# Two 64-wide heads on separate halves of the array in layer two's attention, and its loop written out

## The chip, the cores and the metric

The kernel runs on 1 core of one Trainium2 chip. The metric is the time of one execution on the device in microseconds, the median over runs. Engines are called TensorE (PE; PEld for its weight loads), VectorE (DVE), ScalarE (ACT), GpSimd (POOL) and SyncE (SP, which here issues the DMAs).

## The reference

Two transformer blocks run one after the other on x (256 positions x 2048), all in fp32. The first has two layers: latent attention, then sliding-window attention. The second is one layer with block attention, a state-space mixer and a gated feed-forward network. The change is in the sliding-window layer: 32 query heads of 64 dimensions share 4 key/value heads (8 query heads to one), in two blocks of 128 queries. A query block sees its own keys and those of the block before, within a window of 128, and each head has a sink logit in its softmax.

```python
qb = q.reshape(B, nb, BLOCK, SWA_KV_HEADS, SWA_GROUP, D)
kw, vw = band(k), band(v)
s = jnp.einsum('bnqhgd,bnkhd->bnhgqk', qb, kw).astype(jnp.float32) * (D ** -0.5)
valid = (diff >= 0) & (diff < SWA_WINDOW) & (key_abs >= 0)
s = jnp.where(valid[None, :, None, None], s, NEG_INF)
m = jnp.maximum(jnp.max(s, axis=-1, keepdims=True), sink)
e = jnp.exp(s - m)
p = e / (jnp.sum(e, axis=-1, keepdims=True) + jnp.exp(sink - m))
o = jnp.einsum('bnhgqk,bnkhd->bnqhgd', p.astype(v.dtype), vw)
...
x = x + (y * jax.nn.silu(gate)) @ w_out
```

## The kernel before

**Weight tiles.** All large products stream weights from HBM in tiles of 128 x 1024 fp32. SP loads a tile into one of four slots (`load`, L367), ScalarE casts it to `w_high` (fp32r), VectorE makes the remainder `w_low` (L1458), and TensorE multiplies high by high, high by low and low by high (`block_b`, L445, with 128 x 128 weights and 256 streamed columns; `block_a`, L454). A slot is free when TensorE has used the tile. One tile in the form of `tile_b` is 24 matmuls.

**Layer two.** After the keys and values (L658 to L676) come four projection steps and one step of the output projection. `swa_step(i, project, attend)` (L704) is one: a projection step multiplies 16 tiles (8 for the queries of a group of 8 heads, 8 for their gate) and, placed by hand between the tiles, does the attention of the four head pairs m = 0 to 3 of the group projected in the step before. Step 0 projects only, steps 1 to 3 (the loop at L793) do both, step 4 attends only and has tiles of the output projection in place of the projection's. So 16 pairs are attended, p = 4(i-1) + m. VectorE, ScalarE and POOL run the same steps, with loops of their own (L1779, L1261, L2102), in orders written out by hand.

For each pair TensorE does three things, in this order around the tiles:
- `swa_scores` (L678): for each of the two heads the products of query block 0 with 128 keys and of query block 1 with 256 keys, into that head's own PSUM bank of `sc`, and then one matmul of the identity with the masks (fp32r, 384 columns). The queries of a pair lie in `qs[:, m, :]`, head 0's 64 dimensions on partitions 0 to 63, head 1's on 64 to 127. The keys are placed for each head (`kz`, filled by ScalarE at L1192): head h's 64 partitions hold the keys, the other 64 are zeros (L1661). So each product runs over 128 rows, half of them zeros.
- `probs_transposed` (L516): six transposes of the normalised probabilities, when VectorE has them (`p_ready`).
- `swa_values` (L692): the output of both heads, summed into one bank. `vz`, placed by POOL (L2096), holds head h's values in its 64 of 128 columns and zeros in the others, so head 0's product writes zeros into head 1's output partitions and the other way round, and head 1's is added on top.

The order on TensorE in steps 1 to 3 is scores(0), tiles 0 to 2, flipped(0), tile 3, scores(1), values(0), tiles 4 to 6, flipped(1), tile 7, scores(2), values(1), tiles 8, 9, the rotation of the new queries (four matmuls of 512 columns in all, L740), tile 10, flipped(2), tile 11, scores(3), values(2), tiles 12 to 14, flipped(3), tile 15, values(3). Scores(0) of the next step follows values(3) directly. In step 4 there are two tiles between a scores block, with the values block behind it, and the transposes of the same pair.

All fp32 products and the masks go through one helper, `f32mm` (L485, L486), so they share the line L486 in the profile; they are told apart by their tiles (`scores<-k_swa_placed,q_swa`, `scores<-identity_and_masks`, `bank<-prob_T,v_swa_placed`). Transposes are L489. The softmax of a pair (`row_maxima`, `exponentials`, `normalised` on VectorE and ScalarE) starts on `s_ready`, which the last mask signals.

Layer three (the second block) has in its loop a product `ssm_bcast` (L818) with 16 rows of weights, 128 columns and 512 streamed columns (`bank<-gate,gate_tanh`), and ahead of it one of 33 rows by 8 columns (L816, `bank<-constants,rel_bias`).

Of the kernel before, what the change touches and what calls it, by code (L numbers as in the profile page):

```python
# [31 lines left out]
P = 128  # L32
SEQ = 256
# [117 lines left out]
def after(eng, sem, count):  # L151

    eng.wait_ge(sem, count + 1)
# [23 lines left out]
def program(nc, a, out, toeplitz):  # L177
# [3 lines left out]
    def sb(name, shape, dt=F32, where=None):  # L181
        return (where or persistent).enter_context(nc.sbuf_tensor(name, shape, dt))
# [4 lines left out]
    with ctx:  # L187
# [28 lines left out]
        pT = sb("prob_T", [P, 2, 384], F32, att)  # L216
# [34 lines left out]
        kz = sb("k_swa_placed", [P, SWA_KV, 2, SEQ], F32, a3)  # L251
        vsw = sb("v_swa", [P, TT, SWA_KV * SWA_D], F32, a3)
        vz = sb("v_swa_placed", [P, TT, 2, P], F32, a3)
        qsr = sb("q_swa_raw", [P, 4, SEQ], F32, a3)
        qs = sb("q_swa", [P, 4, SEQ], F32, a3)
# [34 lines left out]
        sc = ctx.enter_context(nc.psum_tensor("scores", [P, 2, 512], F32))  # L290
        b6 = ctx.enter_context(nc.psum_tensor("bank6", [P, 512], F32))
        b7 = ctx.enter_context(nc.psum_tensor("bank7", [P, 512], F32))
        banks = [bank[0][:, :], bank[1][:, :], bank[2][:, :], bank[3][:, :], sc[:, 0, :], sc[:, 1, :],
                 b6[:, :], b7[:, :]]
# [143 lines left out]
        def _(pe):  # L438
# [6 lines left out]
            def block_b(to, tile, cols, chunk, act_h, act_l, first, last):  # L445

                s = tile % SLOTS
                wh, wl = whi[s][:, :], wlo[s][:, :]
                h, l = cols(wh), cols(wl)
                nc.tensor.matmul(to, h, act_h[:, chunk, :], start=first, stop=False, skip_group_check=True)  # L450
                nc.tensor.matmul(to, h, act_l[:, chunk, :], start=False, stop=False, skip_group_check=True)  # L451
                return nc.tensor.matmul(to, l, act_h[:, chunk, :], start=False, stop=last, skip_group_check=True)  # L452

            def block_a(to, tile, cols, chunk, t, act_h, act_l, first, last):  # L454

                s = tile % SLOTS
                h, l = cols(whi[s][:, :]), cols(wlo[s][:, :])
                ah, al = act_h[:, chunk, t * P:(t + 1) * P], act_l[:, chunk, t * P:(t + 1) * P]
                nc.tensor.matmul(to, ah, h, start=first, stop=False, skip_group_check=True)  # L459
                nc.tensor.matmul(to, ah, l, start=False, stop=False, skip_group_check=True)  # L460
                return nc.tensor.matmul(to, al, h, start=False, stop=last, skip_group_check=True)  # L461

            def span(first, n):
                return lambda w: w[:, first:first + n]
# [20 lines left out]
            def f32mm(to, lhsT, rhs, start=True, stop=True):  # L485
                return nc.tensor.matmul(to, lhsT, rhs, start=start, stop=stop, skip_group_check=True)  # L486

            def flip(to, rows_in_):
                return nc.tensor.transpose(to, rows_in_, ident)  # L489
# [40 lines left out]
            for slot, n in enumerate((V_SLOT0, 48, 2 * FC, 2 * FC, 2 * FC, 2 * FC)):  # L530
                last = nc.tensor.transpose(banks[slot // 3][:, (slot % 3) * P:(slot % 3) * P + n], rows[0:n, slot, :], ident[0:n, 0:n])
# [15 lines left out]
            for b in range(4):  # L547
                for c in range(2):
                    for t in range(TT):
                        k = 2 * b + c  # L550
                        last = flip(banks[b][:, c * SEQ + t * P:c * SEQ + (t + 1) * P], c_sb[:, t, k * P:(k + 1) * P])
# [106 lines left out]
            for j in range(8):  # L658
                pe.wait_ge(hl_done, max(8 + j + 1, 8 + 2))
                ready(T_KV + j)  # L660
                for at in range(2):
# [3 lines left out]
                    for t in range(TT):  # L665
                        last = block_a(banks[1][:, t * SEQ:(t + 1) * SEQ], T_KV + j, span(at * 512 + 256, 256), 2 * j + at,
                                       t, hTh, hTl, j + at + t == 0, 2 * j + at == DC - 1)
# [4 lines left out]
            for g in range(SWA_KV):  # L672
                last = f32mm(banks[g][:, 0:SEQ], cst[:, C_DUP + (g % 2) * P:C_DUP + (g % 2 + 1) * P], krot[:, g // 2, :])
# [4 lines left out]
            def swa_scores(i, m):  # L678

                p = 4 * (i - 1) + m  # L680
                after(pe, sw["q_placed"], i)
                after(pe, sw["exp_done"], p)
                after(pe, sw["pt1_sb"], p)
                for h in range(2):
                    for first, q, nk in ((0, 0, P), (P, 1, SEQ)):
                        keys = (kz[:, i - 1, h, 0:nk] if isinstance(i, int) else
                                kz[:, bass.ds(i - 1, 1), h, 0:nk].rearrange("p o n -> p (o n)"))
                        f32mm(sc[:, h, first:first + nk], qs[:, m, q * P:(q + 1) * P], keys, q == 0, False)
                    last = f32mm(sc[:, h, 0:384], ident_r, mask_band, False, True)
                last.then_inc(sw["s_ready"], 1)  # L690

            def swa_values(i, m):  # L692
                p = 4 * (i - 1) + m
                after(pe, sw["pt0_sb"], p + 1)
                after(pe, sw["pt1_sb"], p + 1)
                after(pe, sw["vz"], i)
                after(pe, sw["y32_done"], p)
                for h in range(2):
                    f32mm(banks[7][:, 0:SEQ], vz[:, 0, h, :], pT[:, h, 0:SEQ], h == 0, False)
                for h in range(2):  # L700
                    last = f32mm(banks[7][:, P:SEQ], vz[:, 1, h, :], pT[:, h, SEQ:384], False, h == 1)
                last.then_inc(sw["o_ready"], 1)

            def swa_step(i, project, attend):  # L704
# [19 lines left out]
                def scores(m):  # L724
                    if attend:
                        swa_scores(i, m)
# [5 lines left out]
                def values(m):  # L732
                    if attend:
                        swa_values(i, m)
# [55 lines left out]
                tiles(12, 13, 14, 15)  # L790

            swa_step(0, True, False)
            with pe.Fori(1, 4) as i:  # L793
                swa_step(i, True, True)
            swa_step(4, False, True)
            last_groups(T_SWAO, GROUPS_OUT[1])
# [13 lines left out]
            for c in range(DC):  # L810
                last = block_b(banks[2][:, 0:SEQ], T_DT, span(c * SSM_H, P), c, hTh, hTl, c == 0, c == DC - 1)
# [1380 lines left out]
```

## Time and profile before

| | |
|---|---|
| Median of 3 runs | 2000.13 us (1999.19 to 2002.28) |
| The profiled execution | 2002.27 us, span 2000.1 us |
| TensorE busy | 1907.7 us, 95% of the span, 13112 matmuls |
| VectorE, ScalarE, GpSimd busy | 1110.5, 896.9, 151.3 us |
| Granted clock of TensorE, mean share | 0.982 |
| HBM traffic | 321 MB read, 162 GB/s over the span |
| Layer two, steps 1 to 3 | 486.4 to 673.2 us of the span |

The span is the stretch from the first to the last instruction that the profiler recorded; the execution's own time lies around it. TensorE's matmuls are pipelined, so records of neighbours overlap: a matmul of 256 columns is shown with 0.28 us and the next starts 0.12 us later. What one costs is read from start to start. A row of the time order is: start, duration, engine, line, operation, output<-inputs by the program's names, rows*columns of the weights, the streamed operand, count; several like instructions in a row are merged (x4, x8), and a bracket tells of idle time ahead and of what ended it. A short window shows them singly.

### The profile page before, as it was taken

What the parts mean: (1) busy time and instruction counts of PE and PEld (TensorE: products, weight loads), DVE (VectorE), ACT (ScalarE), POOL (GpSimd) and SP (SyncE); (2) the same over time, 40 slices, a digit from 0 to 9 for tenths busy, and PEclk for the clock granted to TensorE, in tenths of its full rate; (3) what the DMA queues carried; (4) which work ended last, traced back from release to release, by engine and by line L of the source; (5) the groups of instructions that cost most, each with busy time, mean ns of one, the idle gap of its engine ahead of it and who ended that gap; (6) DMA issues with size and microseconds to landing.
All of it is one profiled execution on the core that took longest, in us unless ns stands there. A gap on an engine that the chain in (4) does not pass through costs nothing.

```text
span 2000.1 us, 35228 instructions
## 1 busy us (share of the span) xinstructions
PE 1907.7 (95%) x13112; PEld 1771.1 (89%) x13112; DVE 1110.5 (56%) x1575; ACT 896.9 (45%) x1347; POOL 151.3 (8%) x177
## 2 busy tenths in 40 slices
PE   6899999889999997999999997999999999999997
PEld 5799998789999875999999786999999999988885
DVE  6555565545565655665555555556555556544444
ACT  5454444444444444454344444454444444433333
POOL 1001110000011000000000000100000000023322
PEclk9899999999999998999999998999999999999999
DMA  6455545535444454455554453555556555555553
GB/s 215 144 149 144 154 153 168 168 116 160 146 132 131 127 161 143 127 161 170 157 156 144 163 189 122 183 181 185 181 180 186 179 182 185 180 184 185 187 188 115
DMA packets 234781, 324.11 MB, mean 162 GB/s; under 512 B 12272, under 2 KB 170116, under 8 KB 234080
## 3 DMA queue, kind: packets, MB, share of 16 engines
q1 hardware_dynamic: 233296, 317.63, 51.0%
q0 software_dynamic: 1136, 4.58, 0.7%
q10 hardware_dynamic: 288, 1.09, 0.2%
q8 instruction: 39, 0.64, 0.1%
q14 instruction: 22, 0.18, 0.0%
HBM read 321.14 MB, written 2.11 MB: 162 GB/s over the span
## 4 chain that ended last, share of the span: by engine, by line
PE 92%; DVE 3%; ACT 2%; issue 1%; DMA 1%; POOL 0%; ACTq 0%; DVEq 0%; SPq 0%
PE bank L450 17%; PE bank L451 17%; PE bank L452 17%; PE bank L459 7%; PE bank L461 7%; PE bank L460 7%; PE bank L486 4%; PE bank L1002 3%; PE bank L1001 3%; PE bank L1003 3%; PE scores L486 3%; PE scores L1002 1%; PE scores L1001 1%; PE scores L1003 1%; PE bank L489 1%
## 5 line engine op out<-in xcount | busy, mean ns | idle before, releaser
L1458 DVE TENSOR_TENSOR w_low<-raw,w_high 128x1024 fp32r<-128x1024 f32 x603 | 739.3, 1229 | 756.2 <-ACT w_high L1025 755.7
L1025 ACT CAST w_high<-raw 128x1024 fp32r<-128x1024 f32 x603 | 630.2, 1048 | 828.9 <-PE bank L452 467.5
L450 PE MATMUL bank<-hT_high,w_high 128*128 128x256 f32 x2672 | 765.4, 286 | 8.8 <-issue 3.1
L451 PE MATMUL bank<-hT_low,w_high 128*128 128x256 f32 x2672 | 758.4, 284 | 0.0
L452 PE MATMUL bank<-hT_high,w_low 128*128 128x256 f32 x2672 | 758.4, 284 | 0.0
L450 PEld LDWEIGHTS bank<-hT_high,w_high 128*128 128x128 f32 x2672 | 515.4, 193 | 11.8 <-issue 11.4
L451 PEld LDWEIGHTS bank<-hT_low,w_high 128*128 128x128 f32 x2672 | 515.4, 193 | 1.1 <-issue 1.0
L452 PEld LDWEIGHTS bank<-hT_high,w_low 128*128 128x128 f32 x2672 | 515.2, 193 | 0.0
L459 PE MATMUL bank<-w_high,yT_high 128*128 128x512 f32 x384 | 152.9, 398 | 1.9 <-POOL yT_low L2076 1.9
L461 PE MATMUL bank<-w_high,yT_low 128*128 128x512 f32 x384 | 152.4, 397 | 0.0
L460 PE MATMUL bank<-w_low,yT_high 128*128 128x512 f32 x384 | 151.1, 394 | 0.0
L459 PE MATMUL bank<-w_high,hT_high 128*128 128x256 f32 (+1 forms) x352 | 107.6, 306 | 0.0
L460 PE MATMUL bank<-w_low,hT_high 128*128 128x256 f32 (+1 forms) x352 | 106.4, 302 | 0.0
L461 PE MATMUL bank<-w_high,hT_low 128*128 128x256 f32 (+1 forms) x352 | 106.3, 302 | 0.0
L1001 PE MATMUL bank<-w_high,hidden_high 128*128 128x512 f32 x264 | 104.1, 394 | 1.3 <-DVE up_conv L1994 1.3
L1002 PE MATMUL bank<-w_low,hidden_high 128*128 128x512 f32 x264 | 105.3, 399 | 0.0
L1003 PE MATMUL bank<-w_high,hidden_low 128*128 128x512 f32 x264 | 103.5, 392 | 0.0
L459 PEld LDWEIGHTS bank<-w_high,yT_high 128*128 128x128 f32 x384 | 72.1, 188 | 18.8 <-POOL yT_low L2076 1.6
L461 PEld LDWEIGHTS bank<-w_high,yT_low 128*128 128x128 f32 x384 | 72.1, 188 | 17.5
L460 PEld LDWEIGHTS bank<-w_low,yT_high 128*128 128x128 f32 x384 | 72.1, 188 | 17.4
L459 PEld LDWEIGHTS bank<-w_high,hT_high 128*128 128x128 f32 x352 | 67.2, 191 | 8.5 <-issue 6.1
L461 PEld LDWEIGHTS bank<-w_high,hT_low 128*128 128x128 f32 x352 | 67.2, 191 | 2.5
(270 smaller groups left out, 2022.6 us busy)
## 6 DMA issues: line engine op xcount, KB each, us to landing
raw<-in_w_up SPq DMA_DIRECT2D x176, 512.0 KB, 4.5
raw<-in_w_in SPq DMA_DIRECT2D x88, 512.0 KB, 3.5
raw<-in_w_down SPq DMA_DIRECT2D x88, 512.0 KB, 3.5
raw<-in_w_swa SPq DMA_DIRECT2D x72, 512.0 KB, 3.5
raw<-in_w_c SPq DMA_DIRECT2D x50, 512.0 KB, 3.8
raw<-in_w_mlao SPq DMA_DIRECT2D x32, 512.0 KB, 3.8
raw<-in_w_swao SPq DMA_DIRECT2D x32, 512.0 KB, 4.1
raw<-in_w_out SPq DMA_DIRECT2D x32, 512.0 KB, 3.6
```

Source lines behind the costliest of these rows:

```text
L450: nc.tensor.matmul(to, h, act_h[:, chunk, :], start=first, stop=False, skip_group_check=True)
L451: nc.tensor.matmul(to, h, act_l[:, chunk, :], start=False, stop=False, skip_group_check=True)
L452: return nc.tensor.matmul(to, l, act_h[:, chunk, :], start=False, stop=last, skip_group_check=True)
L459: nc.tensor.matmul(to, ah, h, start=first, stop=False, skip_group_check=True)
L460: nc.tensor.matmul(to, ah, l, start=False, stop=False, skip_group_check=True)
L461: return nc.tensor.matmul(to, al, h, start=False, stop=last, skip_group_check=True)
L486: return nc.tensor.matmul(to, lhsT, rhs, start=start, stop=stop, skip_group_check=True)
L1001: nc.tensor.matmul(to, ah, whi[s][:, w], start=first, stop=False, skip_group_check=True)
L1002: nc.tensor.matmul(to, ah, wlo[s][:, w], start=False, stop=False, skip_group_check=True)
L1003: last = nc.tensor.matmul(to, al, whi[s][:, w], start=False, stop=True, skip_group_check=True)
L1025: nc.scalar.copy(whi[s][:, :], raw[s][:, :]).then_inc(high_made, 1)
L1458: v.tensor_tensor(wlo[s][:, :], raw[s][:, :], whi[s][:, :].bitcast(F32), ALU.subtract).then_inc(low_made, 1)
```

## The change

In `swa_scores` each head's products use only its own 64 partitions of queries and keys (`half`), so 64 rows of the array, and the heads alternate inside each query block; the masks follow both. In `swa_values` each head's product takes only its own 64 columns of `vz` and writes only its own 64 output partitions (`dims`), each with a start of its own. TensorE's loop over steps 1 to 3 becomes Python's, so that its code is written out three times with constant addresses. Nothing else differs: `kz` and `vz` are filled as before, and the other engines keep their loops.

```diff
@@ swa_scores
+                for first, q, nk in ((0, 0, P), (P, 1, SEQ)):
+                    for h in range(2):
+                        half = slice(64 * h, 64 * h + 64)
+                        f32mm(sc[:, h, first:first + nk], qs[half, m, q * P:(q + 1) * P], kz[half, i - 1, h, 0:nk],
+                              q == 0, False)
                 for h in range(2):
-                    for first, q, nk in ((0, 0, P), (P, 1, SEQ)):
-                        keys = (kz[:, i - 1, h, 0:nk] if isinstance(i, int) else
-                                kz[:, bass.ds(i - 1, 1), h, 0:nk].rearrange("p o n -> p (o n)"))
-                        f32mm(sc[:, h, first:first + nk], qs[:, m, q * P:(q + 1) * P], keys, q == 0, False)
                     last = f32mm(sc[:, h, 0:384], ident_r, mask_band, False, True)
                 last.then_inc(sw["s_ready"], 1)
@@ swa_values
                 for h in range(2):
-                    f32mm(banks[7][:, 0:SEQ], vz[:, 0, h, :], pT[:, h, 0:SEQ], h == 0, False)
+                    dims = slice(64 * h, 64 * h + 64)
+                    f32mm(banks[7][dims, 0:SEQ], vz[:, 0, h, dims], pT[:, h, 0:SEQ], True, False)
                 for h in range(2):
-                    last = f32mm(banks[7][:, P:SEQ], vz[:, 1, h, :], pT[:, h, SEQ:384], False, h == 1)
+                    dims = slice(64 * h, 64 * h + 64)
+                    last = f32mm(banks[7][dims, P:SEQ], vz[:, 1, h, dims], pT[:, h, SEQ:384], False, True)
                 last.then_inc(sw["o_ready"], 1)
@@ the steps
             swa_step(0, True, False)
-            with pe.Fori(1, 4) as i:
+            for i in range(1, 4):
                 swa_step(i, True, True)
             swa_step(4, False, True)
```

## Rows read from the trace of the kernel before

**Rows 1.** The page: chain that ended last, share of the span by engine.

```profile
PE 92%; DVE 3%; ACT 2%; issue 1%; DMA 1%; POOL 0%; ACTq 0%; DVEq 0%; SPq 0%
```

**Rows 2.** One pass: length, busy time and count by engine, PEclk, DMA share.

```profile
548.70:610.90 62.20, 62.20 (x486) 60.41 (x485) 38.21 (x75) 28.15 (x63) 6.01 (x10) 1.00 0.44 135
```

**Rows 3.** Who waited for whom, 428 to 745 us: total, times, longest.

```profile
ACT w_high L1025 <- PE bank L452: 90.6, 51, 3.7
...
PE bank L489 <- DVE prob L1507: 5.1, 5, 1.8
...
PE bank L450 <- issue: 3.1, 1, 3.1
```

**Rows 4.** Chain that ended last, 480 to 745: start, us, what.

```profile
500.98 1.67 PE scores L486 x10
502.64 1.31 PE bank L486 x8
```

**Rows 5.** TensorE in order of time, one values block: start, duration, what.

```profile
502.48 0.38 PE L486 MATMUL bank<-prob_T,v_swa_placed 128*128 128x256 f32 x1
...
502.70 0.59 PE L486 MATMUL bank<-prob_T,v_swa_placed 128*128 128x256 f32 x2
...
503.34 0.50 PE L486 MATMUL bank<-prob_T,v_swa_placed 128*128 128x128 f32 x3
...
503.45 0.50 PE L486 MATMUL bank<-prob_T,v_swa_placed 128*128 128x128 f32 x3
```

**Rows 6.** TensorE in order of time, end of one pass, next start.

```profile
547.95 1.47 PE L486 MATMUL bank<-prob_T,v_swa_placed 128*128 128x256 f32 x8
549.25 0.82 PE L486 MATMUL scores<-k_swa_placed,q_swa 128*128 x4
...
550.09 0.82 PE L486 MATMUL scores<-k_swa_placed,q_swa 128*128 x4
...
550.91 0.28 PE L450 MATMUL bank<-hT_high,w_high 128*128 128x256 f32 x1
```

**Rows 7.** In order of time, the 16-row block: TensorE, then its weight loads.

```profile
912.06 0.28 PE L452 MATMUL bank<-hT_high,w_low 128*128 128x256 f32 x1
912.27 1.12 PE L486 MATMUL bank<-gate,gate_tanh 16*128 16x512 f32 x2
913.32 0.39 PE L459 MATMUL bank<-w_high,hT_high 128*128 128x256 f32 x1
913.54 0.28 PE L460 MATMUL bank<-w_low,hT_high 128*128 128x256 f32 x1
...
912.80 0.59 PE L486 MATMUL bank<-gate,gate_tanh 16*128 16x512 f32 x1
...
912.27 0.29 PEld L486 LDWEIGHTS bank<-gate,gate_tanh 16*128 16x128 f32 x2
913.32 0.19 PEld L459 LDWEIGHTS bank<-w_high,hT_high 128*128 128x128 f32 x1 [0.76 <-issue]
```

**Rows 8.** TensorE in order of time, the rotation; its group by line and shape.

```profile
524.57 0.28 PE L452 MATMUL bank<-hT_high,w_low 128*128 128x256 f32 x1
...
526.53 0.28 PE L451 MATMUL bank<-hT_low,w_high 128*128 128x256 f32 x1
...
L486 PE MATMUL bank<-q_swa_raw,constants 128*128 128x512 f32 x16 | 7.5, 592 | 0.0
```

**Rows 9.** TensorE in order of time, the block of 33 rows by 8 columns.

```profile
884.28 0.28 PE L452 MATMUL bank<-hT_high,w_low 128*128 128x256 f32 x1
884.49 0.81 PE L486 MATMUL bank<-constants,rel_bias 33*8 33x384 f32 x2
...
885.45 0.28 PE L451 MATMUL bank<-hT_low,w_high 128*128 128x256 f32 x1
```

**Rows 10.** TensorE in order of time, waits of transposes, first pass and last step.

```profile
497.24 0.55 PE L489 MATMUL bank<-constants,prob 128*128 128x128 f32 x3 [0.32 <-DVE prob L1507]
...
696.99 0.55 PE L489 MATMUL bank<-constants,prob 128*128 128x128 f32 x3 [0.98 <-DVE prob L1507]
```

## The prediction

> **What bounds the kernel now.** I read the page first, then the stretches of layer two, then the chain that ended last inside them, and last TensorE's order of time. The page gives TensorE 92% of the chain that ended last [rows 1]. In layer two the same holds more sharply: the middle one of three like passes lasts 62.2 us and TensorE is busy in all of it, at the full clock of 2.4 GHz (granted share 1.00), while VectorE and ScalarE are busy for some 38 and 28 us [rows 2]. The producers of weight tiles wait for TensorE and not the reverse: ScalarE's cast waits 90.6 us for slots that TensorE frees. TensorE itself waits 5.1 us there, five times, for the normalised probabilities [rows 3]. So a microsecond less on TensorE in a loop pass is a microsecond less in the end, and one more is one more, unless it lies beside those five waits.
>
> The two blocks that change stand in the chain as pieces: a scores block takes 1.67 us, a values block 1.31 [rows 4]. There are 16 of each (pairs 0 to 15), 47.7 us together. That is all the change can touch.
>
> **What a block is made of.** An fp32 product is two TensorE instructions, each with its own weight load: a values block with four products is eight matmuls. Those that stream 256 columns start 0.22 us apart (502.48, 502.70), those of 128 columns 0.11 apart (503.34, 503.45) [rows 5]. So the four products of a values block are 4 x 0.216 + 4 x 0.11 = 1.30. A scores block holds the same number of instructions of the same widths, 1.30, and two masks: a head takes 0.83, its half of the products 0.65, its mask 0.18 [rows 6].
>
> **Part one: changing the array's shape.** The new products use 64 rows (scores) or 64 output columns (values); masks, transposes and weight tiles use the whole array. No row of before has this pair of shapes, but a block in layer three has 16 rows by 128 columns, between two whole-array tiles. From the last whole-array start before it (912.06) to the second one behind it (913.54) is 1.48 us; off go 0.12 each for two ordinary neighbours and 2 x 0.43 for its two matmuls of 512 columns (twice the 0.216 of 256): 0.38, say 0.40 with the roundings [rows 7]. The rotation block of layer two, four such matmuls in the whole array, goes from 524.57 to 526.53, 1.96 us, and 1.96 - 0.24 - 4 x 0.43 = 0.00 [rows 8]. So it is the shape and not the kind of work that costs. It has two halves of 0.20: the load comes 0.21 behind the last start instead of at the next matmul's heels (0.09 of pause, then 0.11 of a load that nothing hides), and the same on the way back (the second matmul begins at 912.80 and streams until 913.23, the load is at 913.32, and the matmul proper, 0.12 ahead of its successor at 913.54, 0.10 later). A block of 33 rows by 8 columns goes from 884.28 to 885.45, 1.17; less 0.24 and 2 x 0.32 (384 columns) leaves 0.29 [rows 9]: with 8 columns to load, the exposed load on the way in is nearly gone, the rest stays. For 64 columns I take the middle, 0.35.
> - Scores: in and out, 16 x 0.40 = 6.4 us (bounds 0.29 to 0.40 a block).
> - Values: in and out, 0.35 a block (0.29 to 0.40).
> - Where values(3) of one pass runs straight into scores(0) of the next, the way out and in is one change and not two: three places, -0.6 us.
>
> The Trainium skill has the same rule ("TensorEngine Tiling (Array Packing)", Key Properties): a change of tiling mode drains TensorE, a change of tile within a mode doesn't. It speaks against this change, and the trace agrees, with the 0.09 pauses above; it gives no price.
>
> **Part two: what the halves may save.** Nothing in the trace of before has two matmuls at once, so this is bounded from both sides: nothing (the products take their 1.30), or half (0.65). Fewer rows alone save nothing: the second 16-row matmul of 512 columns lasts 0.59 [rows 7], the 128-row ones of the rotation 592 ns on average [rows 8]. All that can be saved is saved by running the two heads side by side. Which value I take follows from the order written: both instructions of head 0's product come before both of head 1's, and in every view starts follow program order. So I let a matmul start as soon as the one before it has started and its own half is free. Values: 0, 0.216; head 1 at 0.22, 0.436; then the narrow ones at 0.44, 0.55, 0.65, 0.76, the end at 0.87. That saves 0.43 of 1.30. Scores: by the same rule 0.87, but each of the eight also needs 128 columns of weights, and two loads of 128 columns start no closer than 0.11: the pair of 0.29 in all, of which one lasts 0.18 or 0.19 [rows 7]; a load one by one delays the second half of the stairs, 0, 0.11, 0.22, 0.33, 0.44, 0.656, 0.66, 0.876, the end at 1.09. That saves 0.21. I take 1.09: the loads are spaced 0.11 with 16 rows as with 128. Were loads of different halves made side by side, the scores would end at 0.87 as well; no row shows two loads at once. The loads of values have 64 columns and keep up either way.
>
> The Trainium skill (same page and section) says that different tiles can load weights in parallel. No run here has shown it yet; it is the second of these two cases.
>
> **The sum.** Scores: 0.40 - 0.21 = +0.19 a block, all on the path (the softmax chain starts when they end), 16 x 0.19 = +3.0. Values: 0.35 - 0.43 = -0.08. In the last step three values blocks lie between a scores block and transposes that wait for that same softmax chain, 0.98 us each time [rows 10], so what they gain or lose is swallowed: 13 x -0.08 = -1.0. Merged changes -0.6. **Together +1.4 us.** With loads side by side the scores save 0.43, 16 x -0.03 = -0.5 in place of +3.0, and the sum is -2.1.
>
> The other edits cost nothing. The loop written out: at the pass boundary values(3) starts at 547.95 and scores(0) 1.30 later, with the masks and tiles at their usual distance, so branch and register arithmetic already lie beside matmuls [rows 6]. If fetching longer code stalled TensorE, the one unexplained wait of the stretch, 3.1 us, is my upper bound, and as a gain, were that wait the loop's, it is the lower [rows 3]. I take 0, since the steps before and behind the loop are already written out without such waits. POOL, DVE and ScalarE instructions, DMAs and semaphores are the same; the zeros in the placed keys and values are still written, and nobody waits for them newly. A transposition in a pass has three tiles (8.6 us) and the values block ahead of it and is late but once, by 0.32, where no values block is ahead of it [rows 10]; 0.08 less changes that not at all. If TensorE got much faster, the next to be late would be those same probabilities.
>
> The profiled execution took 2002.27 us around a span of 2000.1; the median of the three runs is 2000.13. The profile is thus at the upper end of them, and I add +1.4 to the median: **2001.5 us** (2003.7 against the profiled one).
>
> **The rivals.**
> - *No overlap.* The halves are used one after the other, because fp32 instructions or the order keep TensorE strictly serial. Products stay at 1.30 and each block pays its change of shape: 16 x 0.40 + 13 x 0.35 - 0.6 = +10.4, **2010.5 us**, slower. Place: every scores block and thirteen values blocks. It decides once overlap saves less than 0.40 in a scores block or 0.35 in a values block. For it: no two matmuls run together anywhere in the trace; the saving needs something never seen here. Against: separate rows or columns hold separate weights, and nothing in the data forbids it. If only one of the kinds overlaps, it is +4.8 (values only: 6.4 - 1.0 - 0.6) or +7.0 (scores only: 3.0 + 4.6 - 0.6).
> - *Stairs with loads side by side.* As above, -2.1, **1998.0 us**. For it: the halves' weights lie apart. Against: loads of few rows and of many are spaced alike.
> - *Full overlap.* Head 1 starts with head 0 whatever was written between: 0.65 saved in both. 16 x (0.40 - 0.65) + 13 x (0.35 - 0.65) - 0.6 = -8.5, **1991.6 us**, faster. For it: the two heads share no half. Against: the order, and starts in program order in every view. The Trainium skill (same page, Theoretical Speedup) speaks of up to twice the speed for a dimension of 64; no row here shows a doubling.
> - *The change doesn't do what it says.* 64 rows or columns run as an idle part of the whole array, no change of shape, no overlap: 0.0, **2000.1 us**. Against: the 16- and 33-row blocks both pay.
>
> **How the numbers follow.** Stairs with loads one by one, the forecast: 0.32 (own range 1999 to 2004, +-1 for roundings and more for the runs' own spread). Stairs with loads side by side: 0.15. No overlap, or in one kind alone: 0.37. Full overlap: 0.11. No change of shape: 0.05. These need 1996 to 2012 for 8 in 10, with full overlap outside. A measurement of this kernel tells apart about 0.2%, 4 us. Both kinds of stairs lie inside that band, as does the unchanged shape; full overlap is faster; no overlap or a single kind is slower. Faster 0.12, same 0.50, slower 0.38.
>
> **What would show it.** In the profile after: matmuls of scores<-k_swa_placed with 64 rows and of bank<-prob_T with 64 columns. Load starts 0.09 late at each change and a first whole-array matmul of 0.39 behind. A scores block of about 1.86 in the chain (0.40 + 1.09 + 0.36) instead of 1.67, a values block of about 1.22 instead of 1.31, and a pass of 62.2 + 4 x 0.19 - 4 x 0.08 - 0.2, some 62.4. No overlap: 2.06 and 1.65, a pass near 65. Full overlap: 1.41 and 1.00, a pass near 59.8. Head 1's first matmul starting while head 0's second still streams is the step on which all hangs. I am wrong if blocks pay no pause, if a pass boundary costs or gains over 0.3 us, or if the transpositions of the passes begin to wait.

## The result and the profile after

The changed kernel takes 1991.69 us (median of 5 runs, 1989.95 to 1994.15), the kernel before in the same series 2002.28 (1999.19 to 2005.20). The ratio is 0.9948, 95% interval 0.9931 to 0.9965: **faster by 0.5%**, some 10 us. The forecast was 2001.5 with a range from 1996 to 2012: wrong, and outside the range. The measured time is that of the rival with full overlap (1991.6), which had a chance of 0.11. That the two agree to 0.1 us is in part luck: the rival counted from a median of 2000.13, and the same kernel has 2002.28 in this series.

The page of the changed kernel: busy time by engine, one DMA queue, the chain by engine.

```profile
PE 1898.3 (95%) x13112; PEld 1748.6 (88%) x13112; DVE 1110.7 (56%) x1575; ACT 895.5 (45%) x1347; POOL 151.5 (8%) x177
...
q8 instruction: 47, 0.77, 0.2%
...
PE 92%; DVE 3%; ACT 2%; issue 1%; DMA 1%; POOL 0%; SPq 0%; DVEq 0%; ACTq 0%
```

TensorE's share of the chain is the same 92% as in [rows 1]; the span fell from 2000.1 to 1991.1 us. The queue that brings instructions has 47 packets where it had 39. That is the loop written out (the run with the loop alone has 47 too), and it shows nowhere else.

Where the time went is read best between two marks that both kernels have: the first rotation matmul of step 0 and the first transpose behind layer two. First the kernel before, then the changed one, the latter with one pass besides, from the second to the third step's rotation (length, busy time and count by engine, PEclk, DMA share, GB/s).

```profile
467.47:797.55 330.08, 311.41 (x2082) 284.51 (x2081) 191.23 (x344) 146.63 (x298) 25.98 (x46) 0.99 0.46 142
```

```profile
467.22:789.24 322.02, 302.02 (x2082) 261.85 (x2081) 191.22 (x344) 145.44 (x298) 26.02 (x46) 0.98 0.48 146
...
583.32:643.30 59.98, 59.97 (x487) 54.93 (x486) 38.18 (x76) 27.87 (x61) 6.03 (x10) 1.00 0.48 141
```

330.08 became 322.02: 8.06 us of the 9.0 of the two profiled spans lie in layer two. The rest comes from outside the change: 0.25 us before the stage and some 0.7 behind it. The mean granted clock doesn't explain it (0.982 before and 0.981 after), and no run shows its cause. A pass is 59.98 us, where it was 62.2 [rows 2].

The chain in the changed kernel, a scores block, the values block behind it and the next tile's first matmul:

```profile
500.72 1.40 PE scores L486 x10
502.13 0.80 PE bank L486 x8
502.93 0.32 PE bank L450
```

1.67 and 1.31 [rows 4] became 1.40 and 0.80; the 0.32 of the first whole-array matmul holds 0.20 that belong to the way out of the values block, so 1.00 in all. The rival had said 1.41 and 1.00.

Now TensorE in order of time in the same place, one short window and its weight loads below it:

```profile
500.44 0.28 PE L452 MATMUL bank<-hT_high,w_low 128*128 128x256 f32 x1
500.65 0.93 PE L486 MATMUL scores<-k_swa_placed,q_swa 64*128 64x128 f32 x8
501.51 0.62 PE L486 MATMUL scores<-identity_and_masks 128*128 128x384 f32 x2
502.06 0.87 PE L486 MATMUL bank<-prob_T,v_swa_placed 128*64 128x256 f32 x8
502.86 0.39 PE L450 MATMUL bank<-hT_high,w_high 128*128 128x256 f32 x1
503.08 0.28 PE L451 MATMUL bank<-hT_low,w_high 128*128 128x256 f32 x1
...
500.65 0.38 PE L486 MATMUL scores<-k_swa_placed,q_swa 64*128 64x128 f32 x2
...
500.65 0.19 PEld L486 LDWEIGHTS scores<-k_swa_placed,q_swa 64*128 64x128 f32 x2
```

Three things are to be seen. The shape has changed (64\*128, 128\*64), and a change looks as in [rows 7]: the last matmul of the tile ends its columns at 500.44 + 0.12 = 500.56, the first load of the new shape comes at 500.65, and a first matmul of 0.39 stands behind the last change. From 500.44 to 503.08 it is 2.64 us for the pair of blocks; in the kernel before the same way took 3.22 (500.69 to 503.91), 0.58 more. The eight score matmuls are over in 0.93 us with their pipeline's tail, where one head's four took 0.82 [rows 6]. And at 500.65 there are two: together they last 0.38, one alone 0.37. Head 1's first matmul starts at once with head 0's first, and so does its load (two loads in 0.19). The records don't name the head; but where both heads use the same half (a run below), the second matmul starts 0.21 behind the first.

Not all that the blocks give back arrives. Read from the last whole-array start before a block or pair of blocks to the second behind it, they take 9.5 us less over layer two (nine pairs of blocks inside the passes 0.58 each, two at a pass boundary 0.76 each, the others 2.8 together), where the stage has 8.06. The rest goes into transposes that wait longer for the probabilities. The first transpose of the third pass, in the kernel before and in the changed one (VectorE's use of the values block's output, with which its work for the next pair begins, and then TensorE's load for the transpose):

```profile
611.71 0.42 DVE L1595 SCALAR_TENSOR_TENSOR y_rows<-bank,gate 128x256 f32<-128x256 f32 x1 [2.06 <-PE bank L486]
...
621.71 0.33 PEld L489 LDWEIGHTS bank<-constants,prob 128*128 128x128 f32 x3
```

```profile
607.00 0.42 DVE L1598 SCALAR_TENSOR_TENSOR y_rows<-bank,gate 128x256 f32<-128x256 f32 x1 [1.56 <-PE bank L486]
...
616.99 0.20 PEld L489 LDWEIGHTS bank<-constants,prob 128*128 128x128 f32 x2 [0.21 <-DVE prob L1510]
```

From the end of the values block, where `y_rows` starts, to that load it is 10.0 us in both (611.71 to 621.71, 607.00 to 616.99): VectorE's and ScalarE's work on the gate, a weight tile and the softmax. Before, TensorE needed just as long for the scores block and three tiles; now its scores block is 0.26 shorter, and it waits. Counted up to the second transpose, each of the three passes loses 0.26, 0.27 and 0.22 us so, and each of pairs 1 to 3 in the last step loses 0.24; together that is 1.5 us. The first transpose of the first pass and one of the last step in the changed kernel (0.32 and 0.98 before, [rows 10]):

```profile
496.99 0.55 PE L489 MATMUL bank<-constants,prob 128*128 128x128 f32 x3 [0.58 <-DVE prob L1510]
...
689.68 0.55 PE L489 MATMUL bank<-constants,prob 128*128 128x128 f32 x3 [1.22 <-DVE prob L1510]
```

### The profile page after: what moved, and what is told of

Read it like the earlier page. It is cut to its first block, busy times and chain, and to the rows that moved or that the text cites. A ratio compares the mean times of both kernels' runs of the same rounds, so it can differ in the third digit from the quotient of the medians.

```text
span 1991.1 us, 35152 instructions
## 1 busy us (share of the span) xinstructions
PE 1898.3 (95%) x13112; PEld 1748.6 (88%) x13112; DVE 1110.7 (56%) x1575; ACT 895.5 (45%) x1347; POOL 151.5 (8%) x177
## 4 chain that ended last, share of the span: by engine, by line
PE 92%; DVE 3%; ACT 2%; issue 1%; DMA 1%; POOL 0%; SPq 0%; DVEq 0%; ACTq 0%
PE bank L450 17%; PE bank L452 17%; PE bank L451 17%; PE bank L459 7%; PE bank L461 7%; PE bank L460 7%; PE bank L1006 3%; PE bank L1005 3%; PE bank L486 3%; PE bank L1004 3%; PE scores L486 3%; PE bank L489 1%; PE scores L1006 1%; PE scores L1005 1%; PE scores L1004 1%
## 5 line engine op out<-in xcount | busy, mean ns | idle before, releaser
L460 PEld LDWEIGHTS bank<-w_low,hT_high 128*128 128x128 f32 x352 | 67.2, 191 | 2.5
```

## The experiments

A pass is always read from the second step's rotation to the third's: 62.25 us in the kernel before by that measure, 59.98 in the changed one.

### Head by head instead of alternating

```diff
-                for first, q, nk in ((0, 0, P), (P, 1, SEQ)):
-                    for h in range(2):
+                for h in range(2):
+                    for first, q, nk in ((0, 0, P), (P, 1, SEQ)):
                         half = slice(64 * h, 64 * h + 64)
...
                 for h in range(2):
                     dims = slice(64 * h, 64 * h + 64)
                     f32mm(banks[7][dims, 0:SEQ], vz[:, 0, h, dims], pT[:, h, 0:SEQ], True, False)
-                for h in range(2):
-                    dims = slice(64 * h, 64 * h + 64)
                     last = f32mm(banks[7][dims, P:SEQ], vz[:, 1, h, dims], pT[:, h, SEQ:384], False, True)
```

> The changed kernel with the heads in turn instead of alternating: head 0's two score products, then head 1's, and the same for values. Theory A (halves work at once, but a product starts only when the one before it has started): stairs come back, head 1's first score product starts 0.22 us behind head 0's first, the products of a scores block end after 0.87 us instead of 0.65, those of a values block after 1.08 instead of 0.65; 16 x 0.22 + 13 x 0.43 = some 9 us more than the changed kernel, near 2001 us. Theory B (each half takes its products on its own, whatever the order written): no difference, 1.40 us a scores block, 60.0 us a pass, near 1991 us.

One pass, and TensorE's order of time in two windows that end 0.01 us apart:

```profile
583.78:643.82 60.04, 60.02 (x487) 55.02 (x486) 38.19 (x76) 27.88 (x61) 6.04 (x10) 1.00 0.48 141
...
501.02 0.37 PE L486 MATMUL scores<-k_swa_placed,q_swa 64*128 64x128 f32 x1
...
501.02 0.39 PE L486 MATMUL scores<-k_swa_placed,q_swa 64*128 64x128 f32 x2
```

60.04 us a pass, 0.06 more than the changed kernel. Head 1's first matmul now stands behind two products of head 0, four matmuls, in the program, and starts within 0.02 us of head 0's first (one matmul of 0.37; one window later two, together 0.39). So starts do not follow the order in which the kernel is written across halves, and the stairs of the forecast fall. Its one run took 1994.37 us. Theory B stands. Whether TensorE itself swaps them or the built program already has them in another order, the records don't say; they have no instruction addresses.

### Both heads on the same half

```diff
-                        half = slice(64 * h, 64 * h + 64)
+                        half = slice(0, 64)
...
-                    dims = slice(64 * h, 64 * h + 64)
+                    dims = slice(0, 64)
```

This leaves out head 1's own scores (it gets head 0's) and the output of 64 partitions. The work on TensorE has the same shapes.

> The changed kernel with both heads on the lower half: 64 rows and partitions 0 to 63 for both (head 1's scores are then head 0's), 64 output partitions 0 to 63 for both in values (the other 64 are left as they are). The same shapes and changes of shape, but nothing can run side by side. Theory A and B (the gain is overlap, the price 0.40 and 0.35 a block): scores block 2.06 us, values block with its way out 1.65, a pass near 65 us, some 10 us over the kernel before, near 2011 us. Rival C (a product of 64 rows or 64 columns is itself faster, or the change of shape is free): a pass of 60 to 62 us, 1991 to 2001 us.

One pass, and two pieces of the chain (start, us):

```profile
588.88:653.80 64.92, 64.92 (x486) 59.17 (x485) 38.27 (x76) 28.25 (x61) 6.00 (x10) 1.00 0.44 130
...
514.67 2.05 PE scores L486 x10
516.73 1.45 PE bank L486 x8
```

64.92 us a pass, 2.05 and 1.45 + 0.20 a block, 2011.84 us, ratio 1.0054 (1.0036 to 1.0071). The *no overlap* rival's numbers (a pass near 65, 2.06, 1.65, 2010.5) hold to 0.1 us a pass. That shows two things at once: products of 64 rows or 64 columns are no faster by themselves, and the price of the shapes is real, +2.67 us a pass. What lies between this run and the changed kernel is overlap alone: a pair of blocks takes 3.93 us here (514.39 to 518.33) and 2.64 there, some 1.3 less, which is a perfect half of its 2.60 us of products. A pass differs by 4.94 us and not by 5.20, since the changed kernel's first transpose waits 0.22 and the one here does not.

### The loop alone

```diff
-            with pe.Fori(1, 4) as i:
+            for i in range(1, 4):
                 swa_step(i, True, True)
```

> Only the loop is written out; all products over the whole array as before. Theory A: no gain and no loss, passes of 62.2 us, ratio to the kernel before 0.999 to 1.001. Rival D (part of the gain is the loop's, in register arithmetic or code fetching at the pass boundaries): passes under 62.0 us or a boundary shorter by over 0.1 us, up to 3 us less in all.

```profile
587.48:649.73 62.25, 62.25 (x487) 60.46 (x486) 38.17 (x76) 28.20 (x61) 6.02 (x10) 1.00 0.46 136
```

Nothing: 62.25 against 62.25, ratio 1.0002 (0.9991 to 1.0014).

### Values alone, scores alone

Values alone (scores as before the change, loop written out):

> Only values in halves, scores over the whole array, loop written out. Theory A: values 0.65 + 0.35 in place of 1.30, in thirteen blocks that count: -3.9 us against the kernel before, a pass of 62.2 - 1.2 = 61.0 us, near 1997 us. Rival E (the two kinds only pay together): no gain, 62.2 us a pass.

```profile
584.90:645.84 60.94, 60.94 (x486) 57.39 (x485) 38.17 (x76) 27.96 (x61) 6.01 (x10) 1.00 0.48 139
```

Scores alone (values as before the change, loop written out):

> Only scores in halves, values over the whole array, loop written out. Theory A: a scores block 0.65 + 0.40 + 0.36 = 1.41 us in place of 1.67, -0.25 in 16 blocks = -4.0 us against the kernel before, a pass of 61.2 us, near 1997 us. Rival E (the two kinds only pay together): no gain, 62.2 us a pass.

```profile
580.32:641.75 61.43, 61.43 (x486) 58.00 (x485) 38.15 (x76) 27.95 (x61) 6.01 (x10) 1.00 0.46 138
```

A pass falls by 1.31 with values alone and by 0.82 with scores alone. The pair of blocks itself, from the last whole-array start before it to the second behind it, with values alone and then with scores alone:

```profile
515.44 0.28 PE L452 MATMUL bank<-hT_high,w_low 128*128 128x256 f32 x1
...
518.34 0.28 PE L451 MATMUL bank<-hT_low,w_high 128*128 128x256 f32 x1
```

```profile
510.25 0.28 PE L452 MATMUL bank<-hT_high,w_low 128*128 128x256 f32 x1
...
513.20 0.28 PE L451 MATMUL bank<-hT_low,w_high 128*128 128x256 f32 x1
```

That is 2.90 and 2.95 us for 3.22 before: a values block has 0.32 less and a scores block 0.27 (0.25 where it stands alone, at the start of step 1), where theory A had 0.30 and 0.25. Four times 0.32 arrive in the pass. Of four times 0.27, some 1.07, it gets only 0.82, because with scores alone too the first transpose of a pass waits for the probabilities (0.20 us before its load at 614.81), and with values alone it does not. The ratios are 0.9962 (0.9948 to 0.9977) and 0.9984 (0.9974 to 0.9995); multiplied they give 0.9946, the whole change 0.9948. The kinds pay each by itself, and rival E falls. Taking 0.65 as saved, the price of the shapes is 0.33 a values block and 0.38 to 0.40 a scores block; the forecast had 0.35 and 0.40.

### How far the look-ahead reaches

The run head by head left open whether order matters at all. So the values products were cut smaller, which leaves the columns streamed by a head the same, 384.

```diff
                 for h in range(2):
                     dims = slice(64 * h, 64 * h + 64)
-                    f32mm(banks[7][dims, 0:SEQ], vz[:, 0, h, dims], pT[:, h, 0:SEQ], True, False)
...
+                    for c in range(0, SEQ, 64):
+                        f32mm(banks[7][dims, c:c + 64], vz[:, 0, h, dims], pT[:, h, c:c + 64], c == 0, False)
+                    for c in range(0, P, 64):
+                        last = f32mm(banks[7][dims, P + c:P + c + 64], vz[:, 1, h, dims], pT[:, h, SEQ + c:SEQ + c + 64],
+                                     False, True)
```

> The changed kernel with a head's two value products cut into six of 64 query columns each, and the heads in turn: all six of head 0 first, then the six of head 1. Theory B (each half takes its products on its own, whatever the order): head 1's first starts some 0.04 us behind head 0's (0.007 us for each product between, as in the run with the heads in turn) and the products end near 0.70 us; a pass of about 60.2 us. Rival B2 (TensorE looks ahead over two products, not over six): head 1 starts 0.3 to 0.65 us behind, the block takes up to 1.3 us, a pass of 61.5 to 62.5 us.

TensorE in three windows with the same beginning, then the block in the chain, then one pass:

```profile
501.11 0.68 PE L486 MATMUL bank<-prob_T,v_swa_placed 128*64 128x64 f32 x8
...
501.11 0.74 PE L486 MATMUL bank<-prob_T,v_swa_placed 128*64 128x64 f32 x9
...
501.11 0.79 PE L486 MATMUL bank<-prob_T,v_swa_placed 128*64 128x64 f32 x10
...
501.18 1.36 PE bank L486 x24
...
585.69:647.89 62.20, 62.19 (x551) 58.14 (x550) 38.19 (x76) 28.11 (x61) 6.03 (x10) 1.00 0.47 136
```

Until 501.62 there are eight matmuls, one after the other, some 0.06 us apart. The window that ends at 501.626 has nine, the one that ends at 501.64 already ten: the tenth is the first of head 1, right behind head 0's ninth of twelve, 0.52 us after the block began (it follows the ninth by 0.01, and the matmuls of one half are 0.06 apart; all sixteen blocks of the run are alike). The block takes 1.36 us and 0.20 for the way out, more than the 1.31 over the whole array, and a pass 62.20, where scores alone had 61.43: the gain of values is gone, and some 0.2 a block with it. Rival B2 is right, and B too simple: there is a look-ahead and it ends. Two further runs asked whether it is a count.

Three products of 128 columns for each head, head by head:

```diff
+                    for c in range(0, SEQ, P):
+                        f32mm(banks[7][dims, c:c + P], vz[:, 0, h, dims], pT[:, h, c:c + P], c == 0, False)
```

> Values in three products of 128 query columns for each head, heads in turn: three of head 0, then three of head 1. With six each, head 1 started 0.52 us late, when one product of head 0 was running and one was waiting; with two each it was 0.013 us late. Theory J (TensorE takes a product for a free half while at most one other product waits ahead of it, four matmuls with the running one): head 1 starts with head 0's second product, 0.22 us late, and the products end at 0.87 us; the block some 0.22 over the changed kernel's, a pass near 60.9 us. Rival K (it is the time or the width, not the count: look-ahead of about half a microsecond): head 1 starts at once, a pass of 60.0 us.

```profile
502.19 0.43 PE L486 MATMUL bank<-prob_T,v_swa_placed 128*64 128x128 f32 x2
...
502.19 0.54 PE L486 MATMUL bank<-prob_T,v_swa_placed 128*64 128x128 f32 x3
...
502.19 0.60 PE L486 MATMUL bank<-prob_T,v_swa_placed 128*64 128x128 f32 x4
...
585.07:646.14 61.07, 61.07 (x502) 56.60 (x501) 38.17 (x76) 27.87 (x61) 6.01 (x10) 1.00 0.47 138
```

Until 502.40 two matmuls, until 502.46 three, and the fourth, head 1's first, before 502.47: right behind head 0's third of six, 0.27 us late. A pass is 61.07 (60.9 expected). In all three runs head 1 started when three matmuls of head 0 were still to start: at once with four in all, behind the third of six, behind the ninth of twelve. Counted in products that is theory J: one product of head 0 runs, one waits, and head 1's is taken. Four in all is only a lower bound, and the two runs with more cut the values alone, so that the reach is shown for halves of the columns; for halves of the rows it is at least as far as two products. Since a product always has two matmuls here, no run tells a count of matmuls from a count of products. Rival K, that half a microsecond is seen ahead, would have started it at once.

Six products each as above, but alternating (`for c ...: for h ...:` in place of the reverse):

> Values in six products of 64 columns for each head as in the run before, but alternating between the heads. Theory J: the order alone made that run slow; here head 1 starts 0.007 us behind head 0, the twelve matmuls of a head stream in 12 x 0.058 = 0.70 us, the block is 0.05 over the changed kernel's 0.80, a pass near 60.2 us. Rival L (short products don't overlap, 64 columns are under what two halves can be fed with): head 1's products delay head 0's, the block stays near 1.36 us, a pass near 62.2 us.

```profile
501.79 0.85 PE bank L486 x24
...
583.22:643.37 60.15, 60.13 (x550) 56.08 (x549) 38.17 (x76) 27.86 (x61) 6.00 (x10) 1.00 0.48 141
```

0.85 and 60.15: the order alone made the difference between 62.20 and 60.15. Short products overlap as well as long ones. Rival L falls.

### A version with fewer changes of shape

```diff
+                if m:
+                    masks(True)
+                    last = products(False)
+                else:
+                    products(True)
+                    last = masks(False)
```

`masks` and `products` are the two parts of `swa_scores`, with the start flag on whichever comes first. For pairs 1 to 3 of a step the masks then follow whole-array tiles, and the score products run straight into the values.

> The changed kernel with the two masks ahead of the score products for pairs 1 to 3 of each step, so that scores in rows of 64 run straight into values in columns of 64: one change of shape in place of two. Theory A (each change costs about 0.2 us, whatever the shapes): nine such places in the passes, -1.8 us against the changed kernel, a pass of 59.4 us instead of 60.0; the three of the last step lie beside the softmax wait. Rival F (only changes from or to the whole array cost): the same or more saved, 0.3 each. Rival G (scores then end later for the softmax or the direct change costs double): no gain, 60.0 us a pass.

One pass, then the chain of a block pair with the masks first and of one at the pass boundary:

```profile
582.54:641.89 59.35, 59.34 (x487) 54.71 (x485) 37.96 (x76) 27.85 (x61) 6.02 (x10) 1.00 0.48 142
...
515.34 1.21 PE scores L486 x10
516.55 0.80 PE bank L486 x8
...
545.76 0.80 PE bank L486 x8
546.56 1.42 PE scores L486 x10
```

1.21 in place of 1.40, and 0.63 less a pass (59.35): three places at some 0.2. The direct way from 64 rows to 64 columns costs one change, as theory A had it. The time: 0.9942 (0.9929 to 0.9955), and once more:

> The kernel with the masks first once more, beside the next one on the same chip. Theory A: ratio to the kernel before 0.9942, as in its first run, 1.9 us under the changed kernel.

0.9934 (0.9920 to 0.9949), 1990.19 us. Both lie below the changed kernel's 0.9948, as the trace says they should, but the intervals overlap: some 1.9 us are 0.1%, which the timed runs can't settle.

Then layer one's rope products (64 dimensions, placed among zeros in `krz`) in halves too; they now come last, behind the masks of that layer:

```diff
+                    for first, q, nk in ((0, 0, P), (P, 1, SEQ)):
+                        for h in range(2):
+                            half = slice(64 * h, 64 * h + 64)
+                            last = f32mm(sc[:, h, first:first + nk], qr[half, q * P:(q + 1) * P], krz[half, h, 0:nk], False, True)
```

> As the kernel with the masks first, and also layer one's rope products (64 dimensions, so far with zeros in the other 64 rows) in halves, head against head: eight blocks of eight products, of which four, 1.30 us, become 0.65 plus 0.40 for in and out. Theory A: -0.25 in each of 8 blocks, -2.0 us more than with the masks first alone. Rival H (layer one waits for something else than TensorE): no difference to it.

Layer one's scores block in the chain of this kernel, then in the changed one:

```profile
150.01 0.33 PE scores L489 x3
...
163.16 2.40 PE scores L486 x18
...
176.52 0.33 PE scores L489 x3
```

```profile
149.53 0.33 PE scores L489 x3
...
162.68 2.86 PE scores L486 x18
...
176.30 0.33 PE scores L489 x3
```

The block has 0.46 less, of which 0.20, the way out, stands with the matmul behind it. From transposes to transposes it is 26.51 us (150.01 to 176.52) in place of 26.77 (149.53 to 176.30): 0.26 less in each of eight blocks, as expected. The runs do not show that at the end: 0.9940 (0.9927 to 0.9954), and again, on the chip of the repeated run above:

> The kernel with layer one's rope products in halves as well, on the same chip as the one with the masks first. Its trace showed 1.8 us less in layer one. Theory A: that arrives at the end, ratio to the kernel before 0.9932. Rival I (later stretches at half clock fall otherwise and swallow it): the same as the one with the masks first, 0.994.

0.9941 (0.9926 to 0.9955). In the first run's trace part of the gain goes right behind layer one: counted from its second transposes, it is 1.8 us ahead of the changed kernel after seven blocks (123.02 to 309.33 us, there 122.27 to 310.40), and at the first rotation of layer two 0.9 are left. In between, from 425 to 445 us, its granted clock is 0.66, between the levels of 1.2 and 2.4 GHz, where the changed kernel has 0.83. That is what rival I says; in the repeated runs both traces have 0.91 there, and still the median with layer one is not the lower one (1990.84 against 1990.19 us). So the fastest versions are these two, with the masks first, at about 0.994; whether layer one adds to it stays open, since nothing was run that would take away what differs between executions around it.

## Why the prediction was wrong

**What bounds the kernel** held in the main: 8.06 of the 9.5 us that the blocks gave back on TensorE arrived in layer two. In one place it was too simple. The forecast's sign of being wrong "if the transpositions of the passes begin to wait" came true: the first of each pass had been just in time, with no room for a shorter scores block ahead of it, and three passes lost 0.75 us together.

**Part one, the shapes,** held. It was called 0.40 a scores block and 0.35 a values block; measured 0.38 to 0.40 and 0.33. The merged changes at the pass boundary held too (values 0.80 straight into scores 1.42 in the last fence of the masks run), and so did the exit of 0.20. The run with both heads on one half came out at 2011.84 us for 2010.5 forecast (ratio 1.0054, some 10.8 us over its own series, for 10.4).

**Part two is the step that failed.** It read: "both instructions of head 0's product come before both of head 1's, and in every view starts follow program order. So I let a matmul start as soon as the one before it has started and its own half is free." No view of before shows neighbouring products on different halves, so a later matmul never had a free part to go to. Program order was a property of that work and was taken for one of the engine. The runs showed in its place: a free half takes its matmul although others, for the busy half, stand ahead of it, as long as no more than three are still to start. The order as written never has more than one product, two matmuls, ahead. So the overlap saved 0.65 us in a block of either kind, and not the 0.21 and 0.43 of the forecast. The second case, loads side by side, was decided as well: the two loads of 500.65 take 0.19 together. The Trainium skill ("TensorEngine Tiling (Array Packing)", Key Properties: tiles operate independently, in loads and matmuls) had both right, and the trace now agrees. Another page of the Trainium skill, "TensorE: Matmul & The Clock Gate" (Part 3: Packing small matmuls), says that matmuls are strictly first in, first out in start and end. That is the rule that the stairs obey; the run with three products each, where head 1's first starts behind head 0's third although three more stand ahead of it, disagrees for products on different halves. The measurement decides.

**The sum.** Forecast +0.19 for a scores block and -0.08 for a values block; measured, each kind alone, -0.27 and -0.32, together -0.58 for a pair of blocks, where the *full overlap* rival had -0.55. Its sum, -8.5, stands against -8.06 in layer two, but two errors meet in that: the blocks gave 9.5 and the waits, which it had at nothing, took 1.5.

**The last step** behaved otherwise than said. The forecast counted thirteen values blocks, since three in the last step should be swallowed. With values alone nothing is: the transposes there wait 0.99 us for 0.98 before, and each follows the one before it 0.3 sooner. With both kinds in halves they wait 1.22, and of 0.57 a pair 0.34 arrive. What sets that limit no run shows. Over all of layer two the idle time of TensorE before these transposes went from 5.1 [rows 3] to 6.1 us:

```profile
PE bank L489 <- DVE prob L1510: 6.1, 5, 1.8
```

**The chances** were wrong too, in one respect that could be seen beforehand. The rival had the mechanism right, and what spoke against it was one sentence, "starts in program order in every view", drawn from views in which the case could not occur. The absence of an overlap in a trace with nothing to overlap is no evidence, and 0.11 was too little for it.

**The loop** cost and gained nothing, as forecast (ratio 1.0002).

## What to carry to other kernels

Work of 64 rows or 64 columns that is padded with zeros to the whole array is worth moving to halves when two such products are at hand: here half of 1.30 us came back for 0.33 to 0.40 of changes of shape, so by that price a block with less than some 0.65 to 0.8 us of such products would not pay. Alternate the halves in the program, or at least keep no more than two fp32 products of one half ahead of the other's, and group what has the same shape so that fewer changes remain. Ask of each wait that isn't there yet how near it is: a transpose that was just in time swallowed most of the 0.26 us of one scores block in four. A price read from other rows (the 16-row and the 33-row block) was good to 0.02 us; a rule on order read from rows in which nothing could have gone otherwise was worth nothing.

## What was not expected of the hardware

- Matmuls start out of the order written when their half of the array is free, with a reach that is a count and not a time: three matmuls of the other half still to start (one product running, one waiting), in blocks of four, six and twelve (late by 0.01, 0.27 and 0.52 us).
- Weight loads of the two halves run at the same time: two in 0.19 us, where two for the same part of the array lie 0.11 apart.
- A change from 64 rows by 128 columns to 128 rows by 64 columns costs one change, not two: some 0.2 us less in each of three places a pass.
- Overlap leaves nothing behind that these traces show: some 1.3 us a pair of blocks between both heads on one half (3.93) and one on each (2.64), of 1.30 for a perfect half.
